# A sandwich of two transformer blocks on one core: the relative-position bias is added by TensorE instead of VectorE

## The reference

```python
def chunked_rel_attention(q, k, v, rel_bias):     # rel_bias: (16, 257)
    s = jnp.einsum('bnihd,bnjhd->bhnij', qc, kb) * scale          # chunks of 64 tokens, 9 chunks in the band
    dist = LEFT_CHUNKS * CHUNK + i[:, None] - j[None, :]
    rel_idx = jnp.clip(dist, -MAX_REL, MAX_REL) + MAX_REL
    s = s + rel_bias[:, rel_idx][None, :, None]
    s = jnp.where(valid[None, None, :, None, :], s, NEG_INF)
    p = jax.nn.softmax(s, axis=-1)
    o = jnp.einsum('bhnij,bnjhd->bnihd', p, vb)
```

## Time and profile before

| | |
|---|---|
| Median of three runs | 2642.25 us (2641.0 to 2642.32) |
| Profiled execution | 2642.25 us, its span 2640.6 us |
| PE busy | 2613.1 us (99%) |
| PEld busy | 2174.4 us (82%) |
| DVE busy | 1422.0 us (54%) |
| ACT busy | 1211.6 us (46%) |
| POOL busy | 98.1 us (4%) |
| DMA | 183 GB/s on average |

### The profile page before, as it was taken

The page is one execution under the profiler, slowest core; times in us unless marked ns, Lnnn a source line. Parts: engine busy times, 40 slices in busy tenths (PEclk is TensorE's granted clock), DMA queues, the critical chain, the costliest instruction groups (busy, mean ns, idle before and its releaser), DMA issues.

```text
span 2640.6 us, 35295 instructions
## 1 busy us (share of the span) xinstructions
PE 2613.1 (99%) x12070; PEld 2174.4 (82%) x12070; DVE 1422.0 (54%) x1687; ACT 1211.6 (46%) x1502; POOL 98.1 (4%) x151
## 2 busy tenths in 40 slices
PE   8999999999999999999999999999999999999998
PEld 6888998888888888888887778888888888888886
DVE  4554655666666664445656555555545454544444
ACT  4444544545455444444544444444444444443443
POOL 0000220000000000002001100000000000000000
PEclk9999999999999999999999999999999999999999
DMA  6655655666666666566666656666666666666654
GB/s 172 176 169 150 164 169 184 183 185 186 185 183 185 184 187 192 187 191 187 199 179 168 175 167 191 189 187 188 184 191 183 192 189 191 190 186 200 196 190 143
DMA packets 358993, 481.99 MB, mean 183 GB/s; under 512 B 22798, under 2 KB 170560, under 8 KB 358784
## 3 DMA queue, kind: packets, MB, share of 16 engines
q1 hardware_dynamic: 353376, 476.27, 60.9%
q0 software_dynamic: 1232, 3.45, 0.6%
q10 hardware_dynamic: 4304, 1.19, 0.2%
HBM read 478.71 MB, written 2.12 MB: 182 GB/s over the span
## 4 chain that ended last, share of the span: by engine, by line
PE 86%; issue 11%; POOL 1%; DVE 1%; ACT 0%; ACTq 0%; POOLq 0%
PE acc L1382 28%; PE acc L1384 28%; PE acc L1383 27%; PE T L1397 1%; PE T L1601 1%; POOL fsq_s L1819 0%; POOL small L1821 0%; PE X L1611 0%; PE X L1716 0%; POOL fqk_s L1824 0%; DVE small L1025 0%; PE T L1696 0%; PE X L1706 0%; ACTq L508 0%; ACT xt_hi L501 0%
## 5 line engine op out<-in xcount | busy, mean ns | idle before, releaser
L833 DVE TENSOR_TENSOR wlo<-raw,whi 128x1024 fp32r<-128x1024 f32 (+1 forms) x916 | 1103.0, 1208 | 997.9 <-ACT whi L483 996.9
L483 ACT ACTIVATE whi<-raw 128x1024 fp32r<-128x1024 f32 (+1 forms) x916 | 950.2, 1044 | 1110.1 <-PE acc L1384 1101.6
L1382 PE MATMUL acc<-whi,xt_hi 128*128 128x512 f32 (+1 forms) x2176 | 842.1, 387 | 3.2 <-DVE wlo L833 3.2
L1384 PE MATMUL acc<-whi,xt_lo 128*128 128x512 f32 (+1 forms) x2176 | 834.4, 383 | 0.0
L1383 PE MATMUL acc<-wlo,xt_hi 128*128 128x512 f32 (+1 forms) x2176 | 834.3, 383 | 0.0
L1382 PEld LDWEIGHTS acc<-whi,xt_hi 128*128 128x128 f32 x2176 | 409.4, 188 | 79.8 <-issue 5.9
L1384 PEld LDWEIGHTS acc<-whi,xt_lo 128*128 128x128 f32 x2176 | 409.2, 188 | 75.5
L1383 PEld LDWEIGHTS acc<-wlo,xt_hi 128*128 128x128 f32 x2176 | 409.5, 188 | 73.8
L1382 PE MATMUL acc<-whi,ht_hi 128*128 128x512 f32 x704 | 277.1, 394 | 0.0
L1384 PE MATMUL acc<-whi,ht_lo 128*128 128x512 f32 x704 | 275.8, 392 | 0.0
L1383 PE MATMUL acc<-wlo,ht_hi 128*128 128x512 f32 x704 | 274.2, 389 | 0.0
(11 more groups left out here) (269 smaller groups left out, 1507.3 us busy)
## 6 DMA issues: line engine op xcount, KB each, us to landing
raw<-in_w_up_dram SPq DMA_DIRECT2D x176, 512.0 KB, 3.7
raw<-in_w_down_dram SPq DMA_DIRECT2D x176, 512.0 KB, 4.7
raw<-in_w_gate_up_dram SPq DMA_DIRECT2D x176, 512.0 KB, 4.3
raw<-in_w_in_dram SPq DMA_DIRECT2D x256, 256.0 KB, 3.3
raw<-in_w_out_dram SPq DMA_DIRECT2D x64, 512.0 KB, 4.0
raw<-in_w_in_dram SPq DMA_DIRECT2D x64, 512.0 KB, 3.7
raw<-in_w_in_dram SPq DMA_DIRECT2D x128, 192.0 KB, 3.0
raw<-in_w_ple_gate_dram SPq DMA_DIRECT2D x32, 512.0 KB, 4.6
```

The lines of the kernel that those rows point to most:

```text
L483: act.activation(whi[:, s, :, 0:w.width], raw[:, s, :, 0:w.width], ACT.Copy).then_inc(hi_made, 1)
L833: dve.tensor_tensor(wlo[:, s, :, 0:w.width], raw[:, s, :, 0:w.width], whi[:, s, :, 0:w.width].bitcast(F32), ALU.subtract).then_inc(lo_made, 1)
L1382: pe.matmul(out_, h_, wh_, start=(j == 0 and kk == 0), stop=False)
L1384: done = pe.matmul(out_, l_, wh_, start=False, stop=(j == w.n - 1 and kk == KS - 1))
```

## The change

The bias is added on TensorE. A matmul with the bias tile as weights and an exchange matrix `anti` (ones where row plus column is 127) as the moving operand gives the tile read backwards, and it accumulates in PSUM on top of the product of q and k. `r_scores` now goes head by head, waits for `btile_made` itself, and waits for X1 and X2 each ahead of its head. `r_maxima` only reduces, straight from PSUM, and `r_softmax` reads PSUM and writes `rp_s`; the banks are given back by ScalarE and not by VectorE. The tile's two kinds change places. GpSimd makes `anti` at the start, and waits for `r_scored` and not for `r_max` before it loads a new tile.

```diff
@@ ScalarE, r_softmax
                 for hh in range(2):
-                    act.activation(rp_s[:, hh, 0:P], rp_s[:, hh, 0:P], ACT.Exp, bias=A_NMX[:, 2 * hh:2 * hh + 1],
+                    act.activation(rp_s[:, hh, 0:P], bank[X1 + hh][:, 0:P], ACT.Exp, bias=A_NMX[:, 2 * hh:2 * hh + 1],
                                    accum_out=A_SUM[:, 2 * hh:2 * hh + 1]).then_inc(r_exp, 1)
-                    act.activation(rp_s[:, hh, P:P + S], rp_s[:, hh, P:P + S], ACT.Exp,
+                    act.activation(rp_s[:, hh, P:P + S], bank[X1 + hh][:, P:P + S], ACT.Exp,
                                    bias=A_NMX[:, 2 * hh + 1:2 * hh + 2],
-                                   accum_out=A_SUM[:, 2 * hh + 1:2 * hh + 2]).then_inc(r_exp, 1)
+                                   accum_out=A_SUM[:, 2 * hh + 1:2 * hh + 2]).then_inc(bank_read[X1 + hh], 1)
@@ VectorE, r_maxima and r_normalise
-            def r_maxima(b, par, use):
-                dve.wait_ge(btile_made, b + 1)
+            def r_maxima(b):
                 for hh in range(2):
                     dve.wait_ge(r_scored, 2 * b + hh + 1)
-                    dve.tensor_tensor(rp_s[:, hh, 0:P], bank[X1 + hh][:, 0:P], btile[:, par, hh, 1, ::-1], ALU.add)
-                    dve.tensor_tensor(rp_s[:, hh, P:P + S].rearrange("p (k t) -> p k t", k=2),
-                                      bank[X1 + hh][:, P:P + S].rearrange("p (k t) -> p k t", k=2),
-                                      btile[:, par, hh, :, ::-1], ALU.add).then_inc(bank_read[X1 + hh], 1)
-                dve.wait_ge(bank_read[X1], USE0[X1]["rel"] + 2 * b + 1)
-                dve.wait_ge(bank_read[X2], USE0[X2]["rel"] + use + 1)
-                for hh in range(2):
-                    dve.tensor_reduce(A_MX[:, 2 * hh:2 * hh + 1], rp_s[:, hh, 0:P], AX.X, ALU.max)
-                    done = dve.tensor_reduce(A_MX[:, 2 * hh + 1:2 * hh + 2], rp_s[:, hh, P:P + S], AX.X, ALU.max)
+                    dve.tensor_reduce(A_MX[:, 2 * hh:2 * hh + 1], bank[X1 + hh][:, 0:P], AX.X, ALU.max)
+                    done = dve.tensor_reduce(A_MX[:, 2 * hh + 1:2 * hh + 2], bank[X1 + hh][:, P:P + S], AX.X, ALU.max)
                 done.then_inc(r_max, 1)
...
-            def r_normalise(b):
-                dve.wait_ge(r_exp, 4 * b + 4)
+            def r_normalise(b, use):
+                dve.wait_ge(bank_read[X2], USE0[X2]["rel"] + use + 1)
@@ TensorE, r_scores
-            def r_scores(b, use):
+            def r_scores(b, par, use):
                 pe.wait_ge(bank_read[T1], USE0[T1]["rel"] + 2 * b + 1)
-                heads = [slice(AD * hh, AD * (hh + 1)) for hh in range(2)]
-                free(X1, "rel", 2 * b)
-                free(X2, "rel", use)
-                for hh, head in enumerate(heads):
-                    pe.matmul(bank[X1 + hh][:, 0:P], rqt_s[head, 0:P], rkt_s[head, 0:P], start=True, stop=True)
-                for hh, head in enumerate(heads):
-                    pe.matmul(bank[X1 + hh][:, P:P + S], rqt_s[head, P:S], rkt_s[head, :], start=True, stop=True).then_inc(r_scored, 1)
+                pe.wait_ge(btile_made, b + 1)
+                for hh in range(2):
+                    free(X1 + hh, "rel", use if hh else 2 * b)
+                    x, head = bank[X1 + hh], slice(AD * hh, AD * (hh + 1))
+                    diagonal, off = btile[:, par, hh, 0, :], btile[:, par, hh, 1, :]
+                    pe.matmul(x[:, 0:P], rqt_s[head, 0:P], rkt_s[head, 0:P], start=True, stop=False)
+                    pe.matmul(x[:, 0:P], diagonal, anti[:], start=False, stop=True)
+                    pe.matmul(x[:, P:P + S], rqt_s[head, P:S], rkt_s[head, :], start=True, stop=False)
+                    pe.matmul(x[:, P:2 * P], off, anti[:], start=False, stop=False)
+                    pe.matmul(x[:, 2 * P:3 * P], diagonal, anti[:], start=False, stop=True).then_inc(r_scored, 1)
@@ GpSimd
+            pool.memset(anti[:], 0.0)
...
+            select(anti[:], ALU.not_equal, 1.0, 1 - P, [[1, P]], 1, const_made)
...
-                for kind, src in ((0, off), (1, diagonal)):
+                for kind, src in ((0, diagonal), (1, off)):
...
-                    pool.wait_ge(r_max, 2 * g + par - 1)
+                    pool.wait_ge(r_scored, 4 * g + 2 * par - 2)
                     btiles(2 * g + par, par)
```

More of the change, by code:

```diff
@@ L177, in sandwich_kernel @@
         ident = sb("ident", [P, P])
+        anti = sb("anti", [P, P])
         ones = sb("ones", [P, S])
@@ L358, in sandwich_kernel @@
         stored = sem("stored")
-        N_CONST = 5
+        N_CONST = 6
         N_LOGIT = 17
@@ L1275, in rel_pieces @@
             def rel_pieces(b, w, last, use, pooled=None):
-                after = {3: [lambda: r_evac(b, w)], 4: [lambda: r_pool(b, w.par)], 5: [lambda: r_maxima(b, w.par, use)],
-                         7: [lambda: r_normalise(b)]}
+                after = {3: [lambda: r_evac(b, w)], 4: [lambda: r_pool(b, w.par)], 5: [lambda: r_maxima(b)],
+                         7: [lambda: r_normalise(b, use)]}
                 if last is not None:
@@ L1720, in rel_pieces @@
             def rel_pieces(b, w, g, use, last=None, pooled=None):
-                after = {1: [lambda: r_turn(b, w, g)], 3: [lambda: r_scores(b, use)], 6: [lambda: r_weights_turn(b)]}
+                after = {1: [lambda: r_turn(b, w, g)], 3: [lambda: r_scores(b, w.par, use)], 6: [lambda: r_weights_turn(b)]}
                 if last is not None:
@@ L1864, in btiles @@
             def btiles(b, par):
-                for kind, src in ((0, off), (1, diagonal)):
+                for kind, src in ((0, diagonal), (1, off)):
                     pool.dma_start(btile[:, par, :, kind, :], src[:, ds(2 * b, 2), :]).then_inc(btile_landed, 16)
                 pool.wait_ge(btile_landed, 32 * b + 32)
-                pool.tensor_tensor(btile[0:AD, par, :, 1, 0:AD], negs[0:AD].rearrange("p (h t) -> p h t", h=2),
+                pool.tensor_tensor(btile[0:AD, par, :, 0, 0:AD], negs[0:AD].rearrange("p (h t) -> p h t", h=2),
                                    ones[0:AD, 0:P].rearrange("p (h t) -> p h t", h=2), ALU.mult).then_inc(btile_made, 1)
```

## The result

The changed kernel takes 2667.18 us (median of 4 runs, 2666.28 to 2667.26) against 2641.95 for the kernel before (4 runs): 25.2 us more, ratio 1.0095 with an interval of [1.0083, 1.0107]. The forecast was 2667.4. That the two lie only 0.2 apart is in part luck, since executions of one kernel differ by about 1 us.

The account below looks back on a forecast made before the run. TensorE's instruction stream was taken to bound the kernel. Per pair 1.31 bias, 0.65 lost overlap and 1.20 row changes gave 3.15, times 8 25.2 us; span 2665.8 plus 1.65 gave 2667.4 us, range 2660 to 2671.5.

Parts of the forecast that it names:

- six bias products: In `r_scores` on TensorE: streaming of the added bias matmuls, 1.31 us a head pair.
- lost overlap of the heads: In `r_scores`: heads no longer next to each other cannot run side by side, 0.65 us a pair.
- six more changes of rows: In `r_scores`: eight switches between 64 and 128 rows instead of two, 1.20 us a pair more.
- relief of VectorE: Additions removed from VectorE, 1.40 us a pair, were hidden and worth 0; rival that 11.2 comes off, 2631: 1%.
- What bounds the kernel: In the phase of the change, TensorE's instruction stream alone sets the time, with nothing left over for waits.
- The price of a change of rows: Each switch between 64-row and 128-row matmuls on TensorE costs 0.20 us, read from `r_scores` and `m_scores`.
- The bounds for the whole: Extra time over eight pairs: 12.4 us with free changes of rows, 31.6 if both weight loads showed after each.
- VectorE's margin: VectorE makes `wlo` of stage 6 1.6 us before TensorE wants it, and that margin grows.
- VectorE's busy time: DVE busy in the profile after would be down by 11 us.
- The new wait on `btile_made`: In `r_scores`, later matmuls stand behind POOL's tile; margin some 40 us, cost 0.
- the longer start: A memset and a select before PE's first matmul, at most 0.49 us, hidden while PE awaits x: cost 0.
- The clock: Granted clock stays 1.00 around `r_scores`; rival that it falls to 1.2 GHz, 21 us more, 2688: 2%.

Follow-up runs that it names:

- experiment 2: Changed kernel with the four q and k products first, both heads side by side, then the six bias products (two changes of rows): 2652.6 us, ratio 1.0041.
- experiment 3: Changed kernel head by head, each head's two q and k products ahead of its three bias products (four changes of rows): 2660.11 us, ratio 1.0071.
- experiment 4: Changed kernel in its own order, but the q and k products take all 128 rows, so no change of rows: 2654.18 us, ratio 1.0048.
- experiment 1: Changed kernel without its six bias products, q and k products in the order of before, VectorE still relieved of its additions: 2641.6 us, ratio 1.0000.
- experiment 5: Kernel before with only the score products reordered, head 0's two, then head 1's two, no bias on TensorE: 2641.78 us, ratio 1.0000.
- experiment 7: Changed kernel in its own order, each bias product on only the 64 rows of its own head: 2654.73 us, ratio 1.0051.

## Why the prediction held, point by point

| Step, per pair | forecast | measured | from |
|---|---|---|---|
| six bias products | 1.31 | 1.34 | experiment 2 against before (2.86 - 1.52) |
| lost overlap of the heads | 0.65 | 0.65 | experiment 3 against 2: 3.90 - 2.86 = 1.04, less two changes at experiment 4's 0.195 (0.39) |
| six more changes of rows | 1.20 | 1.16 | two of them in that 1.04 (0.39), four in experiment 3 (0.77) |
| sum | 3.15 | 3.15 | 4.67 - 1.52 |
| relief of VectorE | 0 | 0 | experiment 1 |

- **What bounds the kernel.** Right: each of these experiments' times follows its piece. The extra of the piece times eight, against the extra of the time: 10.7 and 10.9 (grouped), 19.0 and 18.4 (four changes), 12.7 and 12.4 (all rows), 13.2 and 13.2 (own rows). One step towards it was no proof: the prediction gave `r_output` the 1.05 that were left over, so that its sum had to close. The trace of the kernel before has L1384 at 1375.20 ahead of that piece and L1383 at 1376.67 behind it, 1.47 - 0.46 = 1.01, which bears it out.
- **The price of a change of rows.** Right, 0.19 to 0.20. The bounds for the whole, 12.4 to 31.6 us, were far wider than needed; the value that `r_scores` gave and that `m_scores`, with small fp32 matmuls on both sides of a change, confirmed was the decisive reading.
- **The lost overlap.** Size right, reason not complete ("because the heads no longer stand next to each other"). Experiment 5 puts one head behind the other in the queue and loses nothing. Experiments 2 and 3 show that the loss comes with the bias products between the heads, but not by what: in experiment 3 and in the changed kernel these are 128-row products, they are four to six passes, and the wait for X2 follows them; experiment 7, with no 128-row product, still loses most of its overlap. The cause stays open. Had the change been judged only by the order of the heads, 5.2 us would have been forecast for an edit that costs 0.
- **VectorE's margin.** The conclusion (relief is worth 0) was right; the margin named was the wrong one. The chain goes on from the maxima, through ScalarE's exponentials and `r_normalise`, to `r_weights_turn`, and was tightest there. Had the change made VectorE later instead of earlier, the error would have shown from 0.4 us on.
- **VectorE's busy time** fell by 6.3 us (1422.0 to 1415.7), not by 11. In part this is because the four additions' lengths overlap in the rows, so that the sum of their means overstates what they hold: at the first pair they run from 1361.08 to 1362.23, 1.15 and not 1.40, or 9.2 in all. Of the other 2.9, 0.8 is that the reductions now stand in two groups, which hold 1.24 a pair instead of 1.14, and 0.5 that the 256-column operations of `r_normalise` became longer (347 to 381 ns on average); the rest was not followed up.
- **The new wait on `btile_made` and the longer start** cost nothing: in the phase TensorE waits for no other engine, and its first transposes of x start at 5.37 in both traces.
- **The clock** stayed at 1.00 through the phase, with 2.6 us of streaming in 4.2.

Did the experiments point to a version that beats both? No: the best form of the idea, experiment 2, computes all of it at 2652.6, and even with no bias product at all (experiment 1) the time is that of before.

## What to carry to other kernels

Where one engine's stream has no waits, price a change by that engine's start times alone; work taken off another engine turns into cover. Matmuls that use different numbers of rows should stand in groups: here each change between 64 and 128 rows cost 0.20 us, nearly as much as the small product itself. When naming the cover of a late engine, follow its work to the last consumer, not to the nearest one.

## What the runs showed of the hardware

- TensorE overtakes its own queue. Products of head 1, on rows 64 to 127, started beside head 0's although they stand behind them (experiment 5: at once, with four passes ahead; experiment 7: when four of head 0's ten were left, with a wait for a bank ahead of head 1). The Trainium skill ("TensorE: Matmul & The Clock Gate", Part 3, The mechanism) says that matmuls keep strict queue order in start and end and that only weight loads are pulled ahead; the trace of experiment 7, with L1681 of head 1 ahead of L1684 and L1685 of head 0, disagrees on the starts.
- Each change between products of 64 and of 128 rows cost 0.19 to 0.20 us (experiments 3 and 4). The Trainium skill says that a change of the tiling mode drains TensorE ("TensorEngine Tiling (Array Packing)", Key Properties); the runs agree. Whether head 1 could overtake a single 128-row product is not shown: the least that stood between the heads were four passes of them, five with the one that runs ahead of these, and experiment 7 reached past four in all.
- Reading PSUM instead of SBUF made ScalarE's exponentials no slower: that of 256 columns took 472 ns on average in the phase after the change, 494 before. The read of the accumulated sum behind each grew from 187 ns to between 200 and 205.
